# Two weight pairs per DMA, a shorter lead of the splits, and another order of the last step

## The reference

```
h = rms_norm(x, norm_mix);  x = x + pool_mixer(h)      # causal windows 2, 4, 8, 16, one 256x256 product per group
h = rms_norm(x, norm_ffn)
g = argmax(h @ w_rg + b_rg)                            # 4 groups of 8 experts
two best experts of group g, gates from the softmax
x = x + sum over both of gate * (silu(h @ Wg[e]) * (h @ Wu[e])) @ Wd[e]
out = rms_norm(x, norm_final)
```

## Time and profile before

| | |
|---|---|
| three runs | 660.96, 662.93, 665.18 us |
| the profiled execution: its time | 663.27 us |
| its span | 661.5 us |
| mean granted clock of TensorE | 0.983 |
| TensorE, busy | 622.6 us, 94% |
| VectorE, busy | 606.2 us, 92% |
| ScalarE, busy | 535.7 us, 81% |
| moved by DMA | 242.83 MB, mean 367 GB/s |

### The profile page before, as it was taken

The page is one execution under the profiler, slowest core; times in us unless marked ns, Lnnn a source line. Parts: engine busy times, 40 slices in busy tenths (PEclk is TensorE's granted clock), DMA queues, the critical chain, the costliest instruction groups (busy, mean ns, idle before and its releaser), DMA issues.

```text
span 661.5 us, 9555 instructions
## 1 busy us (share of the span) xinstructions
PE 622.6 (94%) x3460; PEld 526.4 (80%) x3460; DVE 606.2 (92%) x501; ACT 535.7 (81%) x458; POOL 157.9 (24%) x127
## 2 busy tenths in 40 slices
PE   6899989999999999999999999897999989989983
PEld 4799978887888888888888888686877868767872
DVE  5887688989999999999999999897989889998987
ACT  5996626688898989898988988887879688978794
POOL 5000010032222222222222222252225222340311
PEclk9999989999999999999999999999999989989997
DMA  8997769999999999999999999999999999999985
GB/s 293 421 418 278 244 209 374 397 343 302 322 381 404 390 400 393 386 401 374 402 367 401 364 401 366 402 379 392 381 384 386 385 413 384 410 409 400 380 335 211
DMA packets 43637, 242.83 MB, mean 367 GB/s; under 512 B 8184, under 2 KB 9344, under 8 KB 19011
## 3 DMA queue, kind: packets, MB, share of 16 engines
q1 hardware_dynamic: 34322, 220.39, 84.2%
q0 software_dynamic: 9264, 21.79, 12.1%
HBM read 227.19 MB, written 26.21 MB: 383 GB/s over the span
## 4 chain that ended last, share of the span: by engine, by line
DMA 54%; PE 34%; DVE 5%; ACT 3%; issue 2%; SPq 0%; POOL 0%; ACTq 0%; POOLq 0%; DVEq 0%
DMA raw<-in_expert_w_gu 32%; PE psum L1724 19%; DMA raw<-in_expert_w_down 17%; PE psum L1736 3%; PE psum L1652 3%; PE psum L1670 2%; DMA total<-ysb,src_all 2%; PE psum L1638 2%; DMA raw<-total 1%; PE psum L1776 1%; DMA pw_in<-in_pool_w 1%; PE psum L1661 1%; DVE raw L1548 1%; PE psum L1678 1%; PE psum L1787 1%
## 5 line engine op out<-in xcount | busy, mean ns | idle before, releaser
L1210 DVE TENSOR_TENSOR w_lo<-raw,w_hi 128x2048 fp32r<-128x2048 f32 x113 | 255.4, 2284 | 7.8 <-ACT w_hi L884 7.4
L884 ACT ACTIVATE w_hi<-raw 128x2048 fp32r<-128x2048 f32 x113 | 213.5, 1914 | 21.8 <-DMA raw<-in_expert_w_gu 12.8
L1210 DVE TENSOR_TENSOR w_lo<-raw,w_lo 128x2048 fp32r<-128x2048 f32 x79 | 178.5, 2283 | 2.4 <-ACT w_lo L884 2.3
L884 ACT ACTIVATE w_lo<-raw 128x2048 fp32r<-128x2048 f32 x79 | 149.5, 1914 | 13.2 <-DMA raw<-in_expert_w_gu 10.2
L710 POOL DMA_INDIRECT total<-ysb,src_all x28 | 53.5, 1910 | 338.5 <-ACT ysb L979 323.9
L1724 PE MATMUL psum<-w_lo,x_hi 128*128 128x512 f32 x432 | 127.1, 397 | 5.8 <-DVE x_lo L1446 5.8
L1724 PE MATMUL psum<-w_lo,h_hi 128*128 128x512 f32 x376 | 108.3, 395 | 0.5 <-DVE h_lo L1480 0.5
L1724 PEld LDWEIGHTS psum<-w_lo,x_hi 128*128 128x128 f32 x432 | 81.0, 190 | 23.2 <-DVE x_lo L1446 6.7
L696 POOL DMA_INDIRECT xg<-normed,src_all x31 | 78.2, 2523 | 21.5 <-DVE src_all L1305 12.3
L1724 PEld LDWEIGHTS psum<-w_lo,h_hi 128*128 128x128 f32 x376 | 70.9, 190 | 15.5 <-DVE h_lo L1480 0.9
L1736 PE MATMUL psum<-w_lo,x_hi 128*128 128x512 f32 x276 | 74.0, 392 | 0.0
(11 more groups left out here) (208 smaller groups left out, 865.4 us busy)
## 6 DMA issues: line engine op xcount, KB each, us to landing
raw<-in_expert_w_gu SPq DMA_DIRECT2D x128, 1024.0 KB, 10.9
raw<-in_expert_w_down SPq DMA_DIRECT2D x64, 1024.0 KB, 11.8
res<-in_x SPq DMA_DIRECT2D x8, 512.0 KB, 9.7
normed<-nx POOLq DMA_DIRECT2D x8, 512.0 KB, 7.3
total<-res SPq DMA_DIRECT2D x8, 512.0 KB, 8.7
raw<-total SPq DMA_DIRECT2D x8, 512.0 KB, 13.4
out<-raw SPq DMA_DIRECT2D x8, 512.0 KB, 3.9
pw_in<-in_pool_w SPq DMA_DIRECT2D x1, 1024.0 KB, 8.1
```

The costliest lines, as they stand in the source:

```text
L884: nc.scalar.activation(hi_at(s0, j), raw[q][:], ACT.Copy).then_inc(hi_done, 1)
L1210: V.tensor_tensor(w_lo[q][:], raw[q][:], hi_at(s0, j).bitcast(f32), ALU.subtract)\
```

## The change

`GIVEN` loses its second entry, so that from step 4 to the end there are 16 slots and 5 high buffers. From pair 18 on one DMA loads two pairs that follow each other (same expert, same matrix) into two neighbouring slots, with rows of 16 KB; it is issued when both slots are free and the pair four places before its first has landed, and both pairs wait for its one semaphore. `lead(s)` is 2 below step 18 and 1 from there on. Step 31 no longer splits all remaining pairs ahead of the output of expert 29. In step 32 silu, hidden rows and their split come first; squares, norms and the three late additions follow in a new order.

```diff
-    GIVEN = {HEAD: 2, E - 10: 2}
+    GIVEN = {HEAD: 2}
+    LEAN = 18
...
+        raw_two = [at(f"raw_two{q}", [P, 2 * PAIR], f32, 2 * q * SLOT) for q in range(RAW // 2)]
...
-            loads[r] += 1
-            raw_loads.append(16 * loads[r])
+            with_next = m >= RAW
+            raw_sem.append(r - r % 2 if with_next else r)
+            if not (with_next and m % 2):
+                loads[raw_sem[m]] += 1
+            raw_loads.append(16 * loads[raw_sem[m]])
...
-            return min(4, 2 + max(0, s - (E - LATE - 1)))
+            return 2 if s < LEAN else 1
...
-                sp.dma_start(raw[q][:], src[bass.ds(e, 1), :, c * PAIR:(c + 1) * PAIR]
+                n = 1 if pair(s0, j) < RAW else 2
+                where = raw[q] if n == 1 else raw_two[q // 2]
+                sp.dma_start(where[:], src[bass.ds(e, 1), :, c * PAIR:(c + n) * PAIR]
...
-                    if isinstance(s, int) and s >= FREE_STEP:
-                        sp.wait_ge(pair_used, raw_free[pair(s, j)])
-                    elif not (isinstance(s, int) and pair(s, j) < RAW):
-                        sp.wait_ge(pair_used, pair(s, j) - RAW + 1)
+                    if pair(s, j) >= RAW:
+                        if pair(s, j) % 2:
+                            continue
+                        sp.wait_ge(pair_used, raw_free[pair(s, j) + 1])
                     before = pair(s0, j) - FLIGHT
                     if before >= 0:
-                        sp.wait_ge(raw_in[raw_of[before]], landed(before, turn))
+                        sp.wait_ge(raw_in[raw_sem[before]], landed(before, turn))
...
@@ ScalarE, step @@
-                if s == E:
-                    act.wait_ge(pair_used, end_free[TILES // 2])
-                    for i in range(3):
-                        final_square(i, 0)
-                    nc.scalar.activation(warm[:, 1:2], eps[:], ACT.Silu)
...
-                    final_square(3, 0)
                     split_h_block(s - 1, end_free[TILES // 2], hi=h2_hi)
...
                 if s == E - 1:
-                    up_to(split_next, split_pair, s, 2 * PER_STEP)
                     act.wait_ge(pair_used, start(s))
...
@@ ScalarE, after the loop @@
-            for i in range(4, TILES):
+            for i in range(6):
                 final_square(i, 0)
-            for k in range(LATE):
+            for k in range(2):
                 late_squares(k)
+            for i in range(6, TILES):
+                final_square(i, 0)
+            late_squares(2)
...
@@ VectorE, step @@
-                if s == E:
-                    up_to(low_next, low_pair, s, PER_STEP)
-                    dve.wait_ge(nfin_in, 16)
-                    for i in range(3):
-                        final_norm(i, 0)
...
-                    late_add_copied()
-                    final_norm(3, 0)
...
@@ VectorE, after the loop @@
-            for i in range(4, TILES):
+            dve.wait_ge(nfin_in, 16)
+            for i in range(5):
                 final_norm(i, 0)
+            late_add_copied()
             late_add(1, Y, MAIN - GU_PAIRS // 2)
+            for i in range(5, TILES):
+                final_norm(i, 0)
             late_add(2, GU, MAIN)
```

More of the change, by code:

```diff
@@ L119, in hybrid_pool_moe @@
         FIRST = FREE_STEP * PER_STEP - (PER_STEP - GU_PAIRS)
-        raw_of, hi_of, raw_free, hi_free, raw_loads = [], [], [], [], []
+        raw_of, hi_of, raw_free, hi_free, raw_loads, raw_sem = [], [], [], [], [], []
         in_raw, in_hi, loads = [-1] * RAW, [-1] * SPLIT, [0] * RAW
@@ L413, in raw_at, with raw_view @@
             return raw_of[pair(s0, j)]
+        def raw_view(s0, j):
+            q = raw_at(s0, j)
+            return raw[q][:] if pair(s0, j) < RAW else raw_two[q // 2][:, q % 2 * PAIR:(q % 2 + 1) * PAIR]
         def hi_at(s0, j):
@@ L537, in step @@
                             sp.wait_ge(gathered[g], 16)
-                    if isinstance(s, int) and s >= FREE_STEP:
-                        sp.wait_ge(pair_used, raw_free[pair(s, j)])
-                    elif not (isinstance(s, int) and pair(s, j) < RAW):
-                        sp.wait_ge(pair_used, pair(s, j) - RAW + 1)
+                    if pair(s, j) >= RAW:
+                        if pair(s, j) % 2:
+                            continue
+                        assert raw_of[pair(s, j)] % 2 == 0 and raw_of[pair(s, j) + 1] == raw_of[pair(s, j)] + 1
+                        sp.wait_ge(pair_used, raw_free[pair(s, j) + 1])
                     before = pair(s0, j) - FLIGHT
                     if before >= 0:
-                        sp.wait_ge(raw_in[raw_of[before]], landed(before, turn))
+                        sp.wait_ge(raw_in[raw_sem[before]], landed(before, turn))
                     load(s, s0, j, e_up if j < GU_PAIRS else e_down)
@@ L877, in split_pair @@
                 q = raw_at(s0, j)
-                act.wait_ge(raw_in[q], landed(pair(s0, j), turn))
+                act.wait_ge(raw_in[raw_sem[pair(s0, j)]], landed(pair(s0, j), turn))
                 if isinstance(s, int) and s >= FREE_STEP:
@@ L883, in split_pair @@
                     act.wait_ge(pair_used, pair(s, j) - SPLIT + 1)
-                nc.scalar.activation(hi_at(s0, j), raw[q][:], ACT.Copy).then_inc(hi_done, 1)
+                nc.scalar.activation(hi_at(s0, j), raw_view(s0, j), ACT.Copy).then_inc(hi_done, 1)
             act.wait_ge(consts, 1)
@@ L1209, in low_pair @@
                 dve.wait_ge(hi_done, pair(s, j) + 1)
-                V.tensor_tensor(w_lo[q][:], raw[q][:], hi_at(s0, j).bitcast(f32), ALU.subtract)\
+                V.tensor_tensor(w_lo[q][:], raw_view(s0, j), hi_at(s0, j).bitcast(f32), ALU.subtract)\
                     .then_inc(lo_done, 1)
```

## The result

The kernel after takes 673.26 us (median of 4 runs, 671.69 to 673.52), the kernel before beside it 663.84 (4 runs): a ratio of 1.0147, 95% interval 1.0123 to 1.0171. It is slower by 1.5%, outside my range of 656 to 672, and on the side that I gave 0.23. The profiled executions have spans of 671.5 and 661.5 us, so +10.0 us are to be found.

What follows compares the result with a forecast made beforehand. The prediction took the DMA weight stream as the bound (54% of the span, TensorE 34%). Terms +2.3 - 5.3 - 4.4 + 0.5 + 9.3 = +2.4 gave 665.7 us beside the profile's 663.3; range 656 to 672.

Steps and rivals of the forecast that it cites:

- Part 1: Weight stream from pair 18: 87 DMAs of 2 MB with 16 KB rows save fixed packet time, -4.4 us.
- rival C: On the wire, rows still travel in 8 KB packets, so the wide rows gain 0: 670.0, chance 0.20.
- Part 2: Issue of loads until 200 us: both slots must be free, so the even pair goes later, +0.5 us.
- Part 3: Weight stream: two loads in flight instead of four, 2 MB instead of 3 MB left at the next issue, 0 us.
- Rival D: Every 2 MB issue after 200 us: DMA engines run dry with one load left; 682 with no gain, chance 0.08.
- Part 4: Lead 1 from step 18: VectorE's low part of the first pair comes after x, delaying step 28's start, +2.3 us.
- Part 5: Steps 29 to 31: lead no longer grows to 3 and 4, so hidden-row waits and slow clock go, -5.3 us.
- G: End of the last gate/up product on TensorE: 636.6 in the kernel before, forecast 629.7 after.
- Part 6: Second gift of slots (step 22) dropped, five high buffers instead of seven: nothing.
- part 7: Step 31: early split of all pairs gone, copy of expert 29's output ahead of the last splits: nothing.
- Rival E: Scatters and gathers wait behind longer packets, 2.5 us more per scatter; about 668 to 672, chance 0.05.
- Part 8: Last step: silu, hidden and h first, then 11 squares and 11 norms stand in a row, +9.3 us.

Runs made afterwards that it cites:

- wide_flight8: Kernel after with eight pairs in flight (four 2 MB loads) in place of four: 667.65 us, ratio 1.0065 to the kernel before.
- before_flight8: Kernel before with eight 1 MB loads in flight in place of four: 662.85 us, ratio 0.9996.
- narrow_twos: Kernel after with each 2 MB load replaced by two 1 MB loads (8 KB rows) issued together, same waits: 673.24 us, ratio 1.0127 to the kernel before.
- before_flight3: Kernel before with three 1 MB loads in flight in place of four: 665.16 us, ratio 1.0034.
- narrow_left3: narrow_twos without its second wait, so that 3 MB are left when two loads are issued: 672.15 us, ratio 1.0131 to the kernel before.
- before_wide8: Kernel before with 2 MB loads from pair 18, both slots free at issue, and eight pairs in flight: 662.88 us, ratio 1.0.
- after_single: Kernel after with 1 MB loads again, each waiting for its own slot: 666.84 us, ratio 1.0047 to the kernel before.
- before_lead2: Kernel before with lead 2 to the end, no longer 3 and 4: 664.61 us, ratio 1.0022.
- before_wide4: Kernel before with only 2 MB loads from pair 18, both slots free at issue, four pairs in flight: 668.0 us, ratio 1.0071.
- before_new_end: Kernel before with the kernel after's order of the last squares and norms, nothing else: 671.01 us, ratio 1.0111.
- after_lead2: Kernel after with lead 2 in every step: 673.54 us, ratio 1.0144 to the kernel before.

## Why the prediction was wrong, step by step

- **Part 1, the wide rows, −4.4: wrong, and the first half of the failed term.** Rows of 16 KB are there, so rival C is out. But a 16 KB packet takes a median of 611 ns, and two of 8 KB take 2 x 309. Only 7 ns are saved for each pair of rows, and the mean rises, from 2 x 328 to 663 ns between 270 and 440 us. With the depth out of the way, wide_flight8 and before_flight8 land pair 167 at 559.8 and 560.0. The "fixed part of about 11 ns" came from two short stretches, 4 KB rows at 13 to 18 us against 8 KB rows at 605 to 610 us, and I carried it on to a row twice as long in a mixed stream. The term is 0. The Trainium skill ("DMA: Bandwidth & Descriptors", Measured) states that DMAs should be batched to 1 MiB or more for 75% of peak or better. This case shows what lies beyond: past 1 MB, with loads queued behind each other, a larger DMA brought nothing (396 GB/s with 1 MB, 398 with 2 MB). The fit that the prediction took from that page stands in its section "Anatomy of one DMA — SWDGE (gpsimd) path", for DMAs that GpSimd issues; these are SyncE's.
- **Part 2, both slots, +0.5: within its bounds of 0 and 2.9, but taken too near the lower one.** Alone it is 0.5 in the trace of its fastest execution and 2.2 (1.3 to 3.0) by the ratio.
- **Part 3, two in flight instead of four, 0: wrong, the other half.** I had the number of bytes left at an issue, and dismissed it because "the fixed part is small". Parts 1 to 3 together I put at −3.9 at pair 167; they measured +5.3. Part 1 is 4.4 of that gap of 9.2; with 0.5 to 2.2 for part 2, some 3.1 to 4.8 us are left for this part, which I had put at 0. narrow_twos shows that they don't belong to the wide row, before_flight3 that 2 MB left cost 1 MB loads about 2.3 us by the ratio, narrow_left3 that issuing in twos costs something even with 3 MB left, wide_flight8 and before_wide8 that depth cures it. How it divides between the bytes left and the issue in twos stays open.
- **Rival D, the engines run dry: the right place, the wrong mechanism.** I asked for a DMA share clearly below 1. It is 1.01 and 1.00. Counting the packets under way at each moment, between 270 and 440 us 0.13 of 16 engines are free on the mean in the kernel after, 0.02 before: 0.7% of 170 us, 1.2 us. What is lost besides is in the packets: the weights' packets move 24.7 KB (of 1000 bytes) per us each (25.0 before, 24.5 in narrow_twos, 25.5 and 25.7 in before_flight8 and wide_flight8).
- **Part 4, +2.3: right.** TensorE's start of step 28 is 5.3 + 2.3 late, with the low part of 2.27 us where I put it. **Part 5, −5.3: right**; both waits and the slow clock are gone. Together −3.0 in the sum, −3.3 in after_single. With the landing as it was, 2.3 − 5.3 + 5.3 = +2.3, and G came +2.5.
- **Part 6, 0, and part 7, 0: nothing in the traces speaks against them.**
- **Rival E, scatters and gathers behind longer packets: true, and hidden.** The page's part 6 of the kernel after, gathers and then scatters, median us to landing:

```profile
xg<-normed,src_all POOLq DMA_INDIRECT x31, 13.4
...
total<-ysb,src_all POOLq DMA_INDIRECT x28, 11.2
```

  and of narrow_twos, whose times are otherwise as late:

```profile
xg<-normed,src_all POOLq DMA_INDIRECT x31, 10.4
...
total<-ysb,src_all POOLq DMA_INDIRECT x28, 9.9
```

  Counted over the 22 scatters behind 250 us, the median is 10.9 to 12.0 us in the seven kernels with 16 KB rows and 9.2 to 9.9 in the ten with 8 KB rows, whatever the depth; the means are 11.0 to 11.3 and 9.2 to 9.5: about +1.8, where E had 2.5. The scatter of 28 took 13.7 us (12.05 before). It landed at 626.9, and ScalarE's copy at 629.02 follows h at once, so the room that I gave it in part 7 sufficed, with 2.1 us of the 3 left. The Trainium skill ("DMA: Bandwidth & Descriptors", Queues, rings and completion order) states that an engine goes round its queues by packets; by that rule a longer packet in the other queue means a longer turn, and the traces agree with it.
- **Part 8, +9.3: right in its mechanism, 1.8 too large.** With G at 639.15, as in the prediction, h was high at G+4.0 (4.2 predicted), the squares started at G+4.1 (4.7), the first addition ended at G+15.2 (15.9), norm 7 at G+22.4 (23.1). From the squares on all is 0.6 or 0.7 sooner: 0.2 from h, and some 0.3 because the first square comes 0.16 us behind h, where I had 0.5 for reading the overflow count. The rest is behind norm 7, 9.9 us in place of 11.1: the last store landed in 2.99 us, not 4.13.
- **What the parts interact in.** The sum has them add up. The difference can be split that way, −3.3 (leads) + 5.8 (stream, G of after less G of after_single) + 7.5 (end) = +10.0, but each of these is taken in the presence of the others. Alone, in the old order, the traces give +2.2 for the leads (before_lead2, ratio 1.0022), +5.5 for parts 1 to 3 (before_wide4) and +7.3 for the end (before_new_end), together 15.0. The leads bring nothing alone, since that end hangs on the landing of the total. I took G as the start of the tail before; it wasn't. In the new order it is.

The sum was 7.6 us too low: 9.7 too low in the stream, 0.3 and 1.8 too high in the leads and the end. The step that failed is the stream: 4.4 us of gain for the wide rows that measured 0, and nothing for the smaller number of loads in flight, which with both slots measured +5.3. I gave the stream's own risk (rival D) 0.08, and let my range end at 672.

**What stays open.** How the loss of the stream divides between both slots, the bytes left and the issue in twos, and why loads issued together should lose at the same bytes left (after_single against narrow_left3). The rate of the weights' packets between 270 and 440 us mostly goes with the spread of a load's landing over the engines: 24.5 to 24.9 KB per us at a median spread of 2.6 to 3.4 us, 24.9 to 25.0 at 5.5 to 5.9, 25.4 to 25.8 at 8.8 and more. What ties the two together no run here shows, and narrow_left3 falls out of the row: a spread of 6.0 with a rate of only 24.7. Nor do I know why the last landings move by 2 to 3 us with the leads (after_single, before_lead2, after_lead2).

## What to carry to other kernels

Where a stream already runs with its DMA engines full, as here with 1 MB loads at a share of 1.02, ask what a larger DMA could still save; here it was nothing. Look at the depth behind the next issue, and if the unit is doubled let the depth in bytes grow with it (8 pairs in flight made 2 MB loads harmless, 4 cost 5 us together with the wait for both slots).
Before a tail is costed from an event, look for what its first instruction waits for. Here an end of fixed length hung on landings (28.9 to 29.1 us behind the first square, in eight of the nine kernels with the old order), and having the matmuls done 2.3 us sooner by itself didn't bring it forward (before_lead2).
Work in the shadow of a wait was free here; put behind the wait "because the critical engine comes first", it cost 7.3 us, as the engine had nothing else to do while it waited.

## What the runs showed that I had not expected

- A row of 16 KB takes 611 ns, two of 8 KB 618. Above 8 KB the packet's fixed part is hardly to be seen.
- The DMA share can stand at 1.00 to 1.01 while the throughput moves by 4% (381 to 398 GB/s over the same 408 us): a full share says that the engines hold a packet, not how fast it goes.
- The 16 parts of a load land the further apart the more is left at an issue: a median of 2.6 to 3.4 us with 2 MB, 5.5 to 6.0 with 3 MB, 8.8 with 4, 11.2 with 5, 13.7 to 15.8 with 6 and 7 MB. The stream with 5 MB or more left is still no slower.
- 16 KB rows in one queue make the small transfers of the other slower: scatters by about 1.8 us of 9.4 (mean to landing), gathers by 3 of 10.4 (after against narrow_twos).
